# A tuned two-block transformer kernel: another order of quarters ahead of the first seven-product block, weight splits moved to ScalarE, small matmuls in a row, first tiles in front

## The chip, the cores and the metric

The kernel runs on one core of a Trainium2 chip. The metric is device time in microseconds. A core has five engines with instruction queues of their own: TensorE (PE, matmul), VectorE (DVE), ScalarE (ACT), GpSimd (POOL) and SyncE (SP, which only issues DMAs here). Each engine executes its queue in order, and the queues meet through semaphores. 0.2% of this kernel's time is 5.3 us.

## What is computed

Two transformer blocks over 1024 tokens of width 1024, batch 1, all float32.

```python
def first_block(x, ...):
    n = rms_norm(h, attn_norm_w);  proj = n @ w_in          # q, k, v, retention q, k, v, gate
    y_attn = windowed_gqa_sink(rope(norm(aq)), rope(norm(ak)), av, sink)
    y_ret = silu(rg) * rms_norm(bidirectional_retention(rope(rq), rope(rk), rv), ret_norm_w)
    h = h + concat([y_attn, y_ret]) @ w_out
    m = rms_norm(h, ffn_norm_w)
    h = h + (silu(m @ w_gate) * (m @ w_up)) @ w_down        # width 2816

def second_block(h, mem, ...):
    a = rmsnorm(h, g_mix);  proj = a @ w_in                 # 3 x 768 attention, 2 x 512 sgu, 2 x 1024 gates
    y_attn = combine of three dilated windowed attentions
    y_sgu = spatial_gating(...)
    merged = gate0 * (y_attn @ w_branch_attn) + gate1 * (y_sgu @ w_branch_sgu)
    h = h + merged @ w_out
    h = h + cross_attention(rmsnorm(h, g_cross), rmsnorm(mem, g_mem))   # 256 memory tokens
    f = rmsnorm(h, g_ffn)
    h = h + (silu(f @ w_gate) * (f @ w_up)) @ w_down
    return rmsnorm(h, g_final)
```

## The kernel before

**Operands in two parts.** Every large product is made as three matmuls of 128x512: both the weight and the input are split into a high part of type fp32r and the rest (`WH`, `WL`; `XH`, `XL`), and high x high, high x low and low x high are summed in PSUM. So each weight tile costs two splitting operations (high: a copy with rounding; low: a subtraction), on POOL (`split_unit`) or shared between ACT (high) and POOL (low). Inputs are normalised by DVE, split high by ACT and low by DVE or, for the tile numbers in `LOW2` = (5, 7, 9, 10, 11, 13, 14), by POOL. Tile number n is column tile `n % 8` of token half `n // 8`.

**Stages.** In order of time: projections of the first block with windowed attention between them; retention; output projection (`residual`); feed-forward of the first block (`ffn(0, ...)`, first matmuls at about 490 us); the "mix" part of the second block's projections (from about 1137 us); dilated attention, gating and output projection; cross-attention (memory and query units at about 1840 to 1900 us); feed-forward of the second block (`ffn(1, ...)`, from about 1997 us).

**Plain blocks and seven-product blocks.** The feed-forward and the mix part begin with two plain blocks (b = 0, 1): weight block b is cut in quarters A11, A21, A22, A12 of 128x512 and multiplied directly. From b = 2 on a block is done by seven products P1 to P7 instead of eight. They need sums of quarters (`first_sum`: S1 = A21 + A22, into `ACC[:, 1]`; `third_sum`: S3 = A11 - A21, in place of A21; then S2 = S1 - A11 and S4 = A12 - S2, in place of A11 and A12) and sums of the inputs, t1 to t4, which DVE makes and splits with ACT (`input_sums`, semaphores `t_made`, `t_high`, `t_split`). PE takes the products in the order P1, P2, P6, P5, P7, P3, P4, each of 12 matmuls. P1 reads A11, P6 reads S2, P2 reads A12, P5 reads S1, P7 reads S3, P4 reads A22 and P3 reads S4. In the feed-forward, groups of the second weight (`down`) stand between the products from the end of b = 2 on; their raw quarters lie in `XX`.

**The ring of quarters.** Raw quarters are numbered through (`PIECE_OF`, `MIX_PIECE_OF`) and piece r lies in place r % 6: four places in `WRAW`, two in `RAWX`. SP issues the load of piece r once piece r - 6 has been read for the last time (`raw_freed`, `mix_freed`: A11 after S4 and the low part of P6, A21 after the low part of P7, A22 after that of P4, A12 after that of P3; in the plain blocks after the piece's own low part). In the feed-forward the order in which SP issues is sorted by the slot at which the place comes free (`ffn_loads`); in the mix part it is the order of the pieces. SP waits in order, so a load that isn't free yet holds up those behind it. b = 2 has pieces 8 to 11, b = 3 pieces 12 to 15, b = 4 begins with 16.

**POOL's queue at the start of these parts.** `plain` for b = 0: four low parts of weights, then the low parts of the input tiles in `LOW2` (L1010, in the mix part L1182); `plain` for b = 1: four low parts (L986, in the mix part L1131); then for b = 2, at P1: in the feed-forward a wait for `gate_mul` (DVE's first gate), `first_sum` (L1016), `third_sum` (L1022), the low part of P1, S2 (L1050), the low part of P2, and so on; S4 is L1028. After P4 of b = 2: `first_sum` of b = 3, and the sums of the first `down` group (L1064, L1070, L1076). In the mix part the sums of b = 2 come at P1 (L1141, L1147, L1160, L1164) and `mix_first_sum(3)` after P3.

**The cross-attention's weights.** Units of 1024 columns, `CQ_AT[0]` = 73 and `CQ_AT[1]` = 74 for the queries, `MEM_AT[4]` = 72 before them; POOL splits all three, high (L940) and low (L942) for each half. The later units in `EARLY` are shared between ACT, DVE and POOL. `first_units` (L1268, L1269, L1271) starts a pair of units whose inputs are still being made, the second unit three tiles behind the first; `cross_norm` puts the norm's column sums (`norm_sums`, L1284) and its spread over the partitions (`norm_spread`, L1305) between those tiles.

**The very start.** ACT converts three halves of the first two weight units (L2136), then makes `XH` of the first input tiles (L2097, `x_highs`); POOL makes the weights' low parts (L933) and DVE `XL` (L3014).

**The spreads of retention.** `r_spreads(n)` (L1520) spreads the head norms over the partitions, four matmul records for each n; n = 4 to 7 stand between tiles of the output projection's second half (`second_half`), one before each of kt = 0 to 3. DVE then normalises (`r_norms`, L3237, L3239), ACT makes `XH` and DVE `XL` (L3012) of the tiles kt = 4 to 7.

Of the kernel before, what the change touches and what calls it, by code (L numbers as in the profile page):

```python
# [77 lines left out]
EARLY = [MEM_AT[5], CQ_AT[2], MEM_AT[6], MEM_AT[7], CQ_AT[3]]  # L78

# [26 lines left out]
QUARTERS = ("A11", "A21", "A22", "A12")  # L106
GROUPS = ("P1", "P2", "P6", "P5", "P7", "P3", "P4")
# [74 lines left out]
MIX_PIECE_OF = [("plain" if b < 2 else "fast", b, q) for b in range(MIX_BLOCKS) for q in QUARTERS]  # L182
# [11 lines left out]
PIECE_OF = [("plain" if b < 2 else "fast", b, q) for b in range(FT) for q in QUARTERS]  # L194
# [157 lines left out]
def program(nc, xT, memT, ws, vec, cst, rope, bias, wsp, bsg, outT):  # L352
# [6 lines left out]
    with ctx:  # L359
# [564 lines left out]
        def _(pool):  # L924
# [63 lines left out]
            def plain(f, b, u0):  # L988
# [17 lines left out]
                if b == 0:  # L1006
                    for n in LOW2:
                        pool.wait_ge(x_high, (XS_F1, XS_F2)[f] + n + 1)
                        xh, xl = plain_input(n % 8, n // 8)
                        pool.tensor_tensor(xl, scaled_input(n % 8, n // 8), xh.bitcast(F32), ALU.subtract).then_inc(x_low2, 1)  # L1010

            def first_sum(f, b):
                pool.wait_ge(w_low, W_LOW_AT[f] + (SLOT["fast", b - 1, "P5"] + 1 if b > 2 else 8))
                raw_loaded(pool, f, "fast", b, "A21")
                raw_loaded(pool, f, "fast", b, "A22")
                pool.tensor_tensor(S1, raw_of("fast", b, "A21"), raw_of("fast", b, "A22"), ALU.add).then_inc(w_sum, 1)  # L1016
# [13 lines left out]
            def fast(f, b, name):  # L1030
# [3 lines left out]
                if b == 2 and name == "P1":  # L1034

                    pool.wait_ge(gate_mul, 44 * f + 1)
                    first_sum(f, b)
                    third_sum(f, b)
# [110 lines left out]
            def mix_group(b, name):  # L1149
# [3 lines left out]
                if b == 2 and name == "P1":  # L1153
                    mix_first_sum(b)
                    mix_third_sum(b)
# [9 lines left out]
                if name == "P3" and b + 1 < MIX_BLOCKS:  # L1165
                    mix_first_sum(b + 1)
# [4 lines left out]
            for kind, b, name in MIX_SEQ:  # L1171
# [6 lines left out]
                else:  # L1178
                    for n in LOW2:
                        pool.wait_ge(x_high, XS_GMIX + n + 1)  # L1180
                        xh, xl = plain_input(n % 8, n // 8)
                        pool.tensor_tensor(xl, scaled_input(n % 8, n // 8), xh.bitcast(F32), ALU.subtract).then_inc(x_low2, 1)  # L1182
            i = U_FFN1 // 2
# [8 lines left out]
            with pool.Fori(i + 1, EARLY[0] // 2) as i:  # L1192
                for j in range(2):
                    split_unit(i, j)
            split_unit(EARLY[0] // 2, 0)
# [21 lines left out]
        def _(pe):  # L1217
# [321 lines left out]
            def second_half(h, kt):  # L1539
# [3 lines left out]
                if h == 1 and kt < 4:  # L1543
                    r_spreads(4 + kt)
# [424 lines left out]
            def cross_norm(h, kt):  # L1969
                if (h, kt) == (0, 2):  # L1970
# [106 lines left out]
        def _(act):  # L2077
# [55 lines left out]
            for j, q in ((0, 1), (1, 0), (1, 1)):  # L2133
                act.wait_ge(raw_in[j], 16)
                c = slice(512 * q, 512 * q + 512)
                act.activation(WH[:, j, c], WRAW[:, j, c], ACT.Copy).then_inc(one_made, 1)  # L2136

            def x_highs(q):

                act.wait_ge(h_part[q] if q else x_in, 16)  # L2140
                for i in range(4):
                    if (q, i) == (0, 2):
                        act.wait_ge(h_part[0], 16)
# [759 lines left out]
            norm_high(3, 2, 4)  # L2903
            norm_root(3, 1)
            memory_value(4)
            norm_high(3, 4)
            def first_part_high(u):
                i, j = u // 2, u % 2
                act.wait_ge(raw_in[j], 16 * i + 16)
                act.wait_ge(full[2 * j + 1], i)  # L2910
                act.activation(WH[:, j, 0:HALF], WRAW[:, j, 0:HALF], ACT.Copy).then_inc(early_high, 1)
# [74 lines left out]
        def _(dve):  # L2986
# [35 lines left out]
            def norm_step(k, gain, n):  # L3022

                if n < 16:
                    kt, h = n % 8, n // 8
                    if n == 5:
# [773 lines left out]
            norm_step(3, V_GCROSS, 2)  # L3800
            add_squares(3, 15, 1)
            for n in range(3, 17):
                norm_step(3, V_GCROSS, n)

            for n, u in enumerate(EARLY):
                dve.wait_ge(early_high, n + 1)
# [149 lines left out]
```

## Time and profile before

| what | value |
|---|---|
| median of 3 runs | 2663.57 us (2662.53 to 2663.82) |
| the profiled execution's own time | 2663.69 us |
| its span | 2661.9 us |
| PEld, DVE, ACT, POOL busy | 81%, 67%, 42%, 60% |
| chain that ended last | PE 93%, DVE 3%, POOL 1%, issue 1%, ACT 1% |
| mean DMA rate | 65 GB/s |
| `h_spill<-H`, ACT's queue, one issue of 4096 KB | 12.9 us to landing |

The span runs from the first instruction to the last; busy shares are of the span. An engine whose share is near 100% sets the time unless its records hide waits; the chain names what each moment of the span was waiting for. PE's share stands in the rows below.

### The profile page before, as it was taken

How to read it: one execution, taken by the hardware profiler on the slowest of the kernel's cores; microseconds unless marked ns; L12 is line 12 of the kernel's file. 1: busy time of each engine (PE TensorE's matmuls, PEld its weight loads, DVE VectorE, ACT ScalarE, POOL GpSimd, SP SyncE). 2: the span in 40 equal slices, each digit the busy share in tenths (PEclk: the TensorE clock that was granted, in tenths of full speed). 3: DMA queues.
4: the chain of work that ended last, by engine and by line, in shares of the span. 5: the costliest groups of instructions: out<-in, count | busy, mean ns of one | idle time of the engine just before them, and what ended most of it. 6: DMA issues, size and time to landing. Idle time of an engine off the chain costs nothing.

```text
span 2661.9 us, 36644 instructions
## 1 busy us (share of the span) xinstructions
PE 2630.7 (99%) x13442; PEld 2145.0 (81%) x13442; DVE 1777.1 (67%) x2505; ACT 1110.7 (42%) x2152; POOL 1584.5 (60%) x1167
## 2 busy tenths in 40 slices
PE   8999999999999999999999999999999999999998
PEld 6777787878888888878888888888887788888887
DVE  7776775687777777781132447773469877777777
ACT  6644432344444434454443335211445444434443
POOL 3232243478888878667732233557325888878884
PEclk9999999999999999999999999999999999999999
DMA  3111102111121211133211011342101111211112
GB/s 141 33 32 33 45 21 93 55 60 59 57 64 60 64 60 57 55 131 111 85 48 47 25 41 56 134 166 72 64 33 43 58 59 60 72 56 56 60 52 84
DMA packets 110924, 172.98 MB, mean 65 GB/s; under 512 B 7968, under 2 KB 61728, under 8 KB 108576
## 3 DMA queue, kind: packets, MB, share of 16 engines
q1 hardware_dynamic: 100416, 133.20, 15.7%
q10 hardware_dynamic: 10336, 37.49, 3.7%
q8 instruction: 108, 1.77, 0.3%
q14 instruction: 64, 0.52, 0.1%
HBM read 154.93 MB, written 15.73 MB: 64 GB/s over the span
## 4 chain that ended last, share of the span: by engine, by line
PE 93%; DVE 3%; POOL 1%; issue 1%; ACT 1%; DMA 0%; SPq 0%; DVEq 0%; ACTq 0%; POOLq 0%
PE PS L1573 14%; PE PS L1575 14%; PE PS L1574 14%; PE PS L1232 10%; PE PS L1234 9%; PE PS L1233 9%; PE PS L1865 2%; PE PS L1866 2%; PE PS L1867 2%; PE PS L1268 1%; PE PS L1271 1%; PE PS L1269 1%; PE PS L1341 1%; PE PS L1607 1%; PE PS L1367 1%
## 5 line engine op out<-in xcount | busy, mean ns | idle before, releaser
L940 POOL TENSOR_TENSOR WH<-WRAW,CST 128x512 fp32r<-128x512 f32 x150 | 170.9, 1139 | 611.5 <-PE PS L1234 541.3
L1232 PE MATMUL PS<-XH,WH 128*128 128x512 f32 x960 | 395.0, 411 | 0.4 <-DVE XL L3812 0.4
L3509 DVE TENSOR_TENSOR H<-H,PS 128x512 f32<-128x512 f32 x560 | 366.4, 683 | 41.9 <-PE PS L1575 41.8
L1234 PE MATMUL PS<-XH,WL 128*128 128x512 f32 x960 | 376.2, 392 | 0.0
L1233 PE MATMUL PS<-XL,WH 128*128 128x512 f32 x960 | 375.5, 391 | 0.0
L986 POOL TENSOR_TENSOR WL<-WRAW,WH 128x512 fp32r<-128x512 f32 x174 | 260.1, 1496 | 91.1 <-ACT WH L2378 78.0
L986 POOL TENSOR_TENSOR WL<-XX,WH 128x512 fp32r<-128x512 f32 x148 | 197.4, 1335 | 101.9 <-ACT WH L2378 101.5
L1573 PE MATMUL PS<-XH,WH 128*128 128x512 f32 x640 | 249.8, 390 | 1.8 <-ACT ACC L2496 1.4
L1574 PE MATMUL PS<-XL,WH 128*128 128x512 f32 x640 | 249.4, 390 | 0.0
L1575 PE MATMUL PS<-XH,WL 128*128 128x512 f32 x640 | 249.4, 390 | 0.0
L1574 PE MATMUL PS<-PL,WH 128*128 128x512 f32 x624 | 243.2, 390 | 0.0
L1232 PEld LDWEIGHTS PS<-XH,WH 128*128 128x128 f32 x960 | 180.7, 188 | 57.0 <-issue 22.5
L1573 PE MATMUL PS<-PH,WH 128*128 128x512 f32 x576 | 225.0, 391 | 0.7 <-issue 0.7
L1575 PE MATMUL PS<-PH,WL 128*128 128x512 f32 x576 | 224.5, 390 | 0.0
L1234 PEld LDWEIGHTS PS<-XH,WL 128*128 128x128 f32 x960 | 180.4, 188 | 39.3
L942 POOL TENSOR_TENSOR WL<-WRAW,WH 128x512 fp32r<-128x512 f32 x150 | 201.7, 1344 | 11.8
L1233 PEld LDWEIGHTS PS<-XL,WH 128*128 128x128 f32 x960 | 181.1, 189 | 31.5 <-issue 0.5
L1573 PE MATMUL PS<-TR,WH 128*128 128x512 f32 x480 | 187.7, 391 | 3.2 <-DVE ACC L3486 1.7
L1574 PE MATMUL PS<-TR,WH 128*128 128x512 f32 x480 | 187.1, 390 | 0.0
L1575 PE MATMUL PS<-TR,WL 128*128 128x512 f32 x480 | 187.1, 390 | 0.0
L3430 DVE TENSOR_TENSOR PL<-PV,PH 128x512 fp32r<-128x512 f32 x140 | 144.8, 1036 | 38.7 <-ACT PH L2408 38.7
L2408 ACT ACTIVATE PH<-PV 128x512 fp32r<-128x512 f32 x140 | 87.9, 628 | 141.5 <-PE PS L1575 86.1
(456 smaller groups left out, 6087.7 us busy)
## 6 DMA issues: line engine op xcount, KB each, us to landing
WRAW<-ws SPq DMA_DIRECT2D x84, 512.0 KB, 3.4
WRAW<-ws SPq DMA_DIRECT2D x148, 256.0 KB, 2.6
XX<-ws SPq DMA_DIRECT2D x108, 256.0 KB, 2.7
RAWX<-ws SPq DMA_DIRECT2D x68, 256.0 KB, 2.6
gate_spill<-TG ACTq DMA_DIRECT2D x28, 256.0 KB, 2.1
H<-xT ACTq DMA_DIRECT2D x2, 2048.0 KB, 9.6
h_spill<-H ACTq DMA_DIRECT2D x1, 4096.0 KB, 12.9
THB<-gate_spill ACTq DMA_DIRECT2D x4, 1024.0 KB, 5.3
```

The source lines that it names most:

```text
L940: pool.tensor_tensor(WH[:, j, c], WRAW[:, j, c], ONES[:, 0:1].to_broadcast((P, 512)), ALU.mult).then_inc(hi_split, 1)
L942: pool.tensor_tensor(WL[:, j, c], WRAW[:, j, c], WH[:, j, c].bitcast(F32), ALU.subtract).then_inc(unit_split, 1)
L986: pool.tensor_tensor(WLS[:, at], weight(s), WHS[:, at].bitcast(F32), ALU.subtract).then_inc(w_low, 1)
L1232: pe.matmul(out, WH[:, j, w], rh(kt), start=(n == 0), stop=False)
L1233: pe.matmul(out, WH[:, j, w], rl(kt), start=False, stop=False)
L1234: last = pe.matmul(out, WL[:, j, w], rh(kt), start=False, stop=(n == len(kts) - 1))
L1573: pe.matmul(PS[:, bank], WHS[:, at, w], xh, start=start and not on, stop=False, skip_group_check=on)
L1574: pe.matmul(PS[:, bank], WHS[:, at, w], xl, start=False, stop=False, skip_group_check=on)
L1575: return pe.matmul(PS[:, bank], WLS[:, at, w], xh, start=False, stop=stop, skip_group_check=on)
L2408: act.activation(PH[:, n % 2], value(name), ACT.Copy).then_inc(hid_high, 1)
L3430: dve.tensor_tensor(part(name), value(name), PH[:, n % 2].bitcast(F32), ALU.subtract).then_inc(hid_low, 1)
L3509: dve.tensor_tensor(x, x, PS[:, 4 + t], ALU.add).then_inc(h_added, 1)
```

## The change

1. `piece_order`: the quarters of block b = 2 are numbered and loaded in the order A22, A21, A11, A12 (before: A11, A21, A22, A12), in both feed-forwards and the mix part.
2. `first_sum(f, 2)` and `mix_first_sum(2)` move forward in POOL's queue, behind the low part of input tile 7 in the plain block b = 0. They wait for the norm's column sums (`col_sum`) and for A21 and A22. In the mix part, `mix_first_sum(3)` moves from behind P3 to behind P4.
3. In the cross-attention, ACT makes three of the four high halves of units 73 and 74 (`QUERY_HIGHS[1:]`), between its `XH` tiles 2 and 3; POOL keeps one high half and the four low halves. The column sums of the second token half are taken before kt = 4 instead of kt = 2, DVE's last addition of squares comes two tiles later, and its reciprocal at n = 6 instead of 5.
4. `r_spreads(4)` to `r_spreads(7)` stand in a row before kt = 0.
5. At the start ACT makes the first two `XH` tiles before it converts the two halves of the second weight unit.

```diff
+QUERY_HIGHS = [(u, q) for u in CQ_AT[:2] for q in range(2)]
...
+def piece_order(b):
+
+    return ("A22", "A21", "A11", "A12") if b == 2 else QUARTERS
...
-MIX_PIECE_OF = [("plain" if b < 2 else "fast", b, q) for b in range(MIX_BLOCKS) for q in QUARTERS]
+MIX_PIECE_OF = [("plain" if b < 2 else "fast", b, q) for b in range(MIX_BLOCKS) for q in piece_order(b)]
...
-PIECE_OF = [("plain" if b < 2 else "fast", b, q) for b in range(FT) for q in QUARTERS]
+PIECE_OF = [("plain" if b < 2 else "fast", b, q) for b in range(FT) for q in piece_order(b)]
...
                         pool.tensor_tensor(xl, scaled_input(n % 8, n // 8), xh.bitcast(F32), ALU.subtract).then_inc(x_low2, 1)
+                        if n == 7:
+                            first_sum(f, 2)
...
             def first_sum(f, b):
-                pool.wait_ge(w_low, W_LOW_AT[f] + (SLOT["fast", b - 1, "P5"] + 1 if b > 2 else 8))
+                if b > 2:
+                    pool.wait_ge(w_low, W_LOW_AT[f] + SLOT["fast", b - 1, "P5"] + 1)
+                else:
+                    pool.wait_ge(col_sum, 4 + 6 * f)
...
                 if b == 2 and name == "P1":
                     pool.wait_ge(gate_mul, 44 * f + 1)
-                    first_sum(f, b)
                     third_sum(f, b)
...
                 if b == 2 and name == "P1":
-                    mix_first_sum(b)
                     mix_third_sum(b)
...
-                if name == "P3" and b + 1 < MIX_BLOCKS:
+                if name == "P3" and 2 < b < MIX_BLOCKS - 1 or name == "P4" and b == 2:
                     mix_first_sum(b + 1)
...
+                        if n == 7:
+                            mix_first_sum(2)
...
-            with pool.Fori(i + 1, EARLY[0] // 2) as i:
+            with pool.Fori(i + 1, CQ_AT[0] // 2) as i:
                 for j in range(2):
                     split_unit(i, j)
-            split_unit(EARLY[0] // 2, 0)
+            split_unit(CQ_AT[0] // 2, 0)
+            for u, q in QUERY_HIGHS:
+                i, j, c = u // 2, u % 2, slice(512 * q, 512 * q + 512)
+                if (u, q) == QUERY_HIGHS[0]:
+                    pool.wait_ge(raw_in[j], 16 * i + 16)
+                    pool.wait_ge(full[2 * j + 1], i)
+                    pool.tensor_tensor(WH[:, j, c], WRAW[:, j, c], ONES[:, 0:1].to_broadcast((P, 512)), ALU.mult).then_inc(hi_split, 4)
+                    pool.wait_ge(hi_split, 4 * i + 2 * j + 4)
+                else:
+                    pool.wait_ge(early_high, QUERY_HIGHS.index((u, q)))
+                pool.tensor_tensor(WL[:, j, c], WRAW[:, j, c], WH[:, j, c].bitcast(F32), ALU.subtract).then_inc(unit_split, 1)
...
-                if h == 1 and kt < 4:
-                    r_spreads(4 + kt)
+                if (h, kt) == (1, 0):
+                    for n in range(4, 8):
+                        r_spreads(n)
...
-                if (h, kt) == (0, 2):
+                if (h, kt) == (0, 4):
                     norm_sums(3, 1)
...
-            for j, q in ((0, 1), (1, 0), (1, 1)):
+            def first_weights(j, q):
                 act.wait_ge(raw_in[j], 16)
                 c = slice(512 * q, 512 * q + 512)
                 act.activation(WH[:, j, c], WRAW[:, j, c], ACT.Copy).then_inc(one_made, 1)
+            first_weights(0, 1)
...
                     if (q, i) == (0, 2):
+                        first_weights(1, 0)
+                        first_weights(1, 1)
                         act.wait_ge(h_part[0], 16)
...
-            norm_high(3, 2, 4)
+            norm_high(3, 2, 3)
+            for u, q in QUERY_HIGHS[1:]:
+                first_part_high(u, q)
+            norm_high(3, 3, 5)
             norm_root(3, 1)
             memory_value(4)
-            norm_high(3, 4)
+            norm_high(3, 5)
...
-                    if n == 5:
+                    if n == 6:
                         norm_inverse(k, 1)
...
-            norm_step(3, V_GCROSS, 2)
-            add_squares(3, 15, 1)
-            for n in range(3, 17):
+            for n in range(2, 17):
                 norm_step(3, V_GCROSS, n)
+                if n == 4:
+                    add_squares(3, 15, 1)
```

## Rows read from the trace of the kernel before

**Rows 1.** The page, part 1: busy time and share of the span.

```profile
PE 2630.7 (99%) x13442; PEld 2145.0 (81%) x13442; DVE 1777.1 (67%) x2505; ACT 1110.7 (42%) x2152; POOL 1584.5 (60%) x1167
```

**Rows 2.** Waits of PE, whole span: us in total, times, longest us.

```profile
PE PS L1268 <- ACT XH L2097: 8.5, 1, 8.5
```

**Rows 3.** PE by windows: stretch, its us, PE busy (count), clock, DMA share, GB/s.

```profile
545.00:580.00 35.00, 32.16 (x136) 1.00 0.21 69
```

**Rows 4.** PE by windows, the very start.

```profile
8.50:14.90 6.40, 5.94 (x12) 1.00 1.04 389
14.90:22.90 8.00, 8.00 (x37) 1.00 0.87 331
```

**Rows 5.** Timeline, the start: start us, us, engine, line, [idle before <- releaser].

```profile
6.59 1.15 ACT L2136 ACTIVATE WH<-WRAW 128x512 fp32r<-128x512 f32 x2 [0.89 <-DMA WRAW<-ws]
7.65 1.32 ACT L2097 ACTIVATE XH<-H,VEC 128x512 fp32r<-128x512 f32 x2
...
10.11 0.79 PE L1271 MATMUL PS<-XL,WH 128*128 128x512 f32 x1 [0.42 <-DVE XL L3014]
```

**Rows 6.** Timeline, spreads of retention and the last XL behind them.

```profile
396.04 1.89 PE L1520 MATMUL PS<-ROPE,CST 128*64 128x512 f32 x8
...
410.20 1.08 PE L1520 MATMUL PS<-ROPE,CST 128*64 128x512 f32 x4
...
421.82 0.69 DVE L3012 TENSOR_TENSOR XL<-RQ,XH 128x512 fp32r<-128x512 f32 x1 [0.70 <-ACT XH L2097]
```

**Rows 7.** Timeline of POOL in the first feed-forward, blocks 2 and 3.

```profile
530.45 1.29 POOL L1016 TENSOR_TENSOR ACC<-WRAW,RAWX 128x512 f32<-128x512 f32 x1 [7.68 <-DVE SQ L3418]
...
535.88 1.53 POOL L986 TENSOR_TENSOR WL<-WRAW,WH 128x512 fp32r<-128x512 f32 x1 [2.70 <-ACT WH L2378]
...
551.88 2.98 POOL L986 TENSOR_TENSOR WL<-RAWX,WH 128x512 fp32r<-128x512 f32 x2
555.49 1.67 POOL L1016 TENSOR_TENSOR ACC<-WRAW 128x512 f32<-128x512 f32 x1 [0.63 <-DVE SQ L3418]
...
566.88 1.74 POOL L986 TENSOR_TENSOR WL<-WRAW,WH 128x512 fp32r<-128x512 f32 x1
```

**Rows 8.** Timeline of DVE and PE, same stretch.

```profile
555.94 1.78 DVE L3447 TENSOR_TENSOR PV<-SQ,PV 128x512 f32<-128x512 f32 x1
...
560.07 0.50 PE L1573 MATMUL PS<-TR,WH 128*128 128x512 f32 x1 [0.87 <-DVE ACC L3486]
...
568.76 0.47 PE L1573 MATMUL PS<-XH,WH 128*128 128x512 f32 x1 [0.24 <-POOL WL L986]
```

**Rows 9.** DMA issue at 554.9 us: size, us to landing.

```profile
RAWX<-ws SPq DMA_DIRECT2D x1, 256.0 KB, 4.2
```

**Rows 10.** DMA issue at 2062.1 us, the same piece in the second feed-forward.

```profile
RAWX<-ws SPq DMA_DIRECT2D x1, 256.0 KB, 3.1
```

**Rows 11.** Timeline of POOL and PE in the mix part, first plain block.

```profile
1152.00 1.27 POOL L1182 TENSOR_TENSOR XL<-SC,XH 128x512 fp32r<-128x512 f32 x1 [3.36 <-ACT XH L2097]
1155.68 1.29 POOL L1182 TENSOR_TENSOR BXL<-SC,BXH 128x512 fp32r<-128x512 f32 x1 [2.40 <-ACT BXH L2097]
...
1157.27 0.39 PE L1832 MATMUL PS<-BXL,WH 128*128 128x512 f32 x1
```

**Rows 12.** DMA issue at 1147.0 us, piece 9 of the mix part.

```profile
WRAW<-ws SPq DMA_DIRECT2D x1, 256.0 KB, 10.3
```

**Rows 13.** DMA issue at 1203.2 us, the first after P4's low part.

```profile
RAWX<-ws SPq DMA_DIRECT2D x1, 256.0 KB, 3.4
```

**Rows 14.** Timeline of POOL and PE in the mix part, blocks 2 and 3.

```profile
1197.73 0.51 PE L1865 MATMUL PS<-TR,WH 128*128 128x512 f32 x1 [1.57 <-DVE TR L3399]
...
1204.39 1.30 POOL L1131 TENSOR_TENSOR WL<-WRAW,WH 128x512 fp32r<-128x512 f32 x1
...
1209.54 0.39 PE L1865 MATMUL PS<-XH,WH 128*128 128x512 f32 x1
```

**Rows 15.** Timeline of PE, the cross-attention's first query units.

```profile
1862.91 0.50 PE L1268 MATMUL PS<-XH,WH 128*128 128x512 f32 x1 [0.63 <-POOL WL L942]
```

More of the change, by code:

```diff
@@ L2900, in _, with first_part_high @@
                     act.activation(MH[:].rearrange("p a b -> p (a b)"), XX[:], ACT.Copy).then_inc(mem_high, 1)
-            norm_high(3, 2, 4)
+            def first_part_high(u, q=0):
+                i, j, c = u // 2, u % 2, half(q)
+                act.wait_ge(raw_in[j], 16 * i + 16)
+                act.wait_ge(full[2 * j + 1], i)
+                act.activation(WH[:, j, c], WRAW[:, j, c], ACT.Copy).then_inc(early_high, 1)
+            norm_high(3, 2, 3)
+            for u, q in QUERY_HIGHS[1:]:
+                first_part_high(u, q)
+            norm_high(3, 3, 5)
             norm_root(3, 1)
             memory_value(4)
-            norm_high(3, 4)
[L2907 to L2911, printed above, removed]
+            norm_high(3, 5)
             for n in range(4):
@@ L3798, in _ @@
                     last.then_inc(mem_val, 1)
-            norm_step(3, V_GCROSS, 2)
-            add_squares(3, 15, 1)
-            for n in range(3, 17):
+            for n in range(2, 17):
                 norm_step(3, V_GCROSS, n)
+                if n == 4:
+                    add_squares(3, 15, 1)
             for n, u in enumerate(EARLY):
-                dve.wait_ge(early_high, n + 1)
+                dve.wait_ge(early_high, 3 + n + 1)
                 dve.tensor_tensor(WL[:, u % 2, 0:HALF], WRAW[:, u % 2, 0:HALF], WH[:, u % 2, 0:HALF].bitcast(F32),
```

## Prediction

> **What bounds the kernel.** The page's busy line first: PE is busy for 2630.7 of 2661.9 us [rows 1], so the kernel is a string of matmuls, and what an edit can win is PE's idle time, 31 us in all. Two lumps of it are not for this change to win whole: the 8.5 us before the first matmul [rows 2] and the tail. Next the waits of PE and its windows: the idle time between sits where a stage begins. The start of the first feed-forward's fast blocks has 35.0 - 32.16 = 2.8 us [rows 3], the second feed-forward repeats it, the mix part has 1.6 us in one wait [rows 14], and the cross-attention some 1.3, of which the longest stands in [rows 15]. A term of this forecast is therefore a microsecond or two, and its sign depends on who is late next.
>
> **The start (edit 5).** ACT converts two weight halves from 6.59 us and only then makes XH at 7.65, since the input had just come (its own idle time is none there) [rows 5]; so XH itself hardly moves (0.1 us). What moves is POOL: those two halves' low parts no longer run beside the first XL, and PE waits for that XL, until 10.11 [rows 5]. A DVE operation on SBUF beside a POOL one takes 1.78 us [rows 8] where the plain ones beside nothing take 0.69 [rows 6], so the first XL comes 1.0 us earlier. PE then works at its lower rate: 12 matmuls in 6.4 us up to 14.9 us, about 35 in the next 8 [rows 4]; 0.43 us each are 512 columns at 1.2 GHz, 0.23 us nearly that at 2.4 GHz, although the clock column has no lower grant for that stretch. If the clock still rises at 14.9, a start 1.0 us earlier puts two more matmuls before the rise, and each is worth 0.23 us afterwards: -0.5 us, not -1.0. Bounds: -1.1 (the rise comes with the work) and +0.2 (the third and fourth XL now meet POOL's low parts). The Trainium skill ("TensorE: Matmul & The Clock Gate", Part 1) says that the monitor behind the clock runs free of the kernel's start, so that the rise is not tied to the first matmul; by that rule the term could be -0.5 in one run and -1.1 in another, and no row here tells which.
>
> **The spreads in a row (edit 4).** Four records between other matmuls take 1.08 us, eight in a row 1.89 [rows 6]: four more cost 0.81 to 0.85, so sixteen in a row take 3.6 where four times four take 4.1. Each break also costs PE about 0.1 us on either side (a first matmul behind a wait or another kind lasts 0.50 instead of 0.39 [rows 8, 14]), and three of four breaks go. Together 0.5 + 0.6 = 1.1 us. But the last tile's XL starts at 421.82 and ends at 422.5 [rows 6], at the end of a ladder of DVE and ACT steps that begins with the first spread at 410.20 and doesn't get earlier. PE uses that XL at 422.95 now; 1.1 us earlier it would wait for it. So 0.3 us is won. Bounds -1.1 and 0.
>
> **The cross-attention (edit 3).** POOL loses three conversions of about 1.04 us. PE waits 0.63 us for one of its low parts [rows 15], and two shorter waits before it are DVE's and ACT's. But three ACT conversions of 0.6 us now stand before the XH of tile 3, and the low halves that remain on POOL still run beside DVE's XLs. I place tile 2's XL about 1 us earlier, tile 4's and 5's at the same time as now, since the column sums with ACT's root and DVE's reciprocal move behind them. The spread that follows starts 0.2 to 0.6 us earlier: -0.4 us. Bounds: -1.9 (all waits and their refills) and +0.7 (three conversions, less the 1.1 us of slack that XH of tile 3 has).
>
> **The first sum (edits 1 and 2), first feed-forward.** What goes: one POOL operation of 1.29 us at 530.45, behind 7.68 us of idle time. POOL idles for another 2.70 us afterwards, until ACT delivers at 535.88 [rows 7]. So nothing waits for it, and taking it away wins nothing; at its new place (about 505 us) POOL is idle too. What is added is a load that comes later. Piece 14 (A22 of b = 3) lies in place 14 % 6 = 2, which was A11's of b = 2, free at S4; it is now A22's, free at the low part of P4, POOL's second operation of the pair at 551.88, so at 554.86 [rows 7]. In SP's sorted order it goes last of seven, where a load issued at that moment takes 4.2 us [rows 9]: landed at 559.07. POOL's `first_sum(3)` reads it, now at 555.49 [rows 7]: 3.6 us late, and behind it in POOL's queue stand the two `down` sums and the low parts for which PE waits, with 0.24 us of idle time at 568.76 [rows 8], where POOL's string has no slack. How much reaches PE? The string from 555.49 to the low part at 566.88 is 8 operations, most of them 1.57 to 1.75 us because DVE works beside them [rows 7]; free they take 1.29 [rows 7]. While POOL waits for the load, DVE is free and runs ahead (its 1.78 us operation at 555.94 [rows 8] becomes 0.7, and PE's wait of 0.87 us at 560.07 [rows 8] goes), so that most of the string then runs uncontended: I count three operations contended and five free, -1.7 us, and 0.7 us of slack at the `down` group behind. 3.6 - 1.7 - 0.7 = +1.2 us. Bounds +0.3 (all eight free) and +3.4 (all contended as now).
>
> **Second feed-forward.** The same, but there the load takes 3.1 us [rows 10], 1.1 less: +0.1 us, bounds -0.2 and +2.4.
>
> **The mix part.** (a) `mix_first_sum(2)` now stands behind the low part at 1152.00, with idle time until 1155.68 [rows 11]. It needs pieces 8 and 9. Piece 9 is issued at 1147.0 and takes 10.3 us [rows 12], beside the 4 MB spill of H: landed at 1157.3. So POOL waits for the load until 1157.3, then 1.29 for the sum and 1.29 for the low part of tile 9, which is ready at 1159.9; PE uses it at 1157.27 [rows 11]. That is 2.6 us, 2.7 with the refill. Behind it PE has 1.57 us of idle time at 1197.73, until DVE's t-splits arrive [rows 14], which the delay fills: +1.1 us, if DVE's chain stays where it is (one POOL operation less beside its sums, but all the others later). Bounds 0 and +2.7. (b) Piece 14 again: issued when P4's low part ends at about 1203.1, 3.4 us to land [rows 13], then `first_sum(3)`, the third sum and P1's low part, 3 x 1.29: 1210.4 instead of 1205.7 (1204.39 + 1.30); PE starts P1 at 1209.54 [rows 14]. 0.9 and a refill of 0.1: +1.0 us. Bounds 0 (POOL's queue is shorter and PE later by a) and +2.2. (a) is the risk that the moved sum creates: a wait for a load in front of low parts that PE needs at once.
>
> **The sum.** -0.5 - 0.3 - 0.4 + 1.2 + 0.1 + 1.1 + 1.0 = +2.2 us, against the profiled execution: 2663.7 + 2.2 = 2665.9. That execution lies 0.1 us above the median of the three runs (2663.57), so the forecast for a median is 2665.8 us. +2.2 us is 0.08%. What this kernel's measurement can tell from no change is about 0.2%, 5.3 us, so I call this no change.
>
> **Rivals.** (A) *The late load decides.* POOL's string in both feed-forwards keeps its contended durations, the delay of `first_sum(3)` reaches PE whole (+3.4 and +2.4), and in the mix part DVE's chain moves with PE (+2.7, +2.2): 10.7, less 1.2 for the other edits: +9.5, 2673.1 us. It decides from about 1.5 us per feed-forward on. For it: POOL's string reaches PE with 0.24 us of idle time now; against: DVE's operations run in the gap. Slower by 0.36%. (B) *The covers hold and the small edits pay.* The loads' delays vanish in slack, and start (-1.0), spreads (-1.1), cross-attention (-1.9) come through: -4.0, with 1.0 left for the mix part: -3.0, 2660.6 us. For it: PE's idle time is there to win; against: each of the three has its next waiter named above. Faster by over 0.2% it would be only from -5.3 us on. (C) *Nothing arrives.* The first sum had 2.70 us of slack where it stood and the new load order costs nothing that PE sees; the first sum is not the wait at all: 2663.4 us.
>
> **How the numbers follow.** Forecast 0.45, A 0.15, B 0.2, C 0.2. The time is 2665.8. The range takes in B and C and the lower half of the way to A: 2660.3 to 2670.2. Slower by over 0.2% (2668.9 and more): A whole and a little of the forecast's upper bounds, 0.17. Faster by over 0.2% (below 2658.2): B with every bound at its end, 0.07. Within: 0.76.
>
> **What would show it.** PE starts with its third matmul near 9.4 us and no 0.42 us wait. The spreads stand as 16 records in about 3.6 us, with a new PE wait of about 0.5 us for XL near 421.8. POOL has no L1016 between 522 and 530 us; a gap of about 4 us ended by a DMA stands before `first_sum(3)` in both feed-forwards, and PE's idle time in the stretch of [rows 3] grows by about 1 us. In the mix part a POOL gap ended by `WRAW<-ws` near 1157, then a PE wait of about 2.6 us for BXL, and a shorter or no wait for L3399 near 1198; a PE wait for POOL before P1 of b = 3. Wrong would be: no PE wait at BXL (then piece 9 landed earlier or the order of the queue isn't what I read), or PE's idle time in the feed-forward's stretch smaller than before.

## The result, and the profile after

| | before | after |
|---|---|---|
| median, the two timed side by side | 2664.29 us (13 runs) | 2670.45 us (13 runs) |
| ratio to before | 1 | 1.0021, 95% interval 1.0014 to 1.0028 |
| the profiled execution | 2663.69 us, span 2661.9 | 2669.91 us, span 2668.1 |

The change makes the kernel slower, by 6.2 us by the medians and 5.6 us by the ratio. Page part 1 of the kernel after answers to [rows 1]: PE is busy for 2.5 us more, though it runs the same 13442 matmuls.

```profile
PE 2633.2 (99%) x13442; PEld 2148.4 (81%) x13442; DVE 1766.5 (66%) x2505; ACT 1112.2 (42%) x2155; POOL 1574.6 (59%) x1164
```

Waits of PE of the kernel after (line waited at, releaser: us in total, times, longest). Two kinds are new, 6.3 and 3.3 us:

```profile
PE PS L1597 <- POOL WL L994: 6.3, 2, 3.2
PE PS L1856 <- POOL BXL L1193: 3.3, 1, 3.3
```

PE by windows (stretch, its us, PE busy and count, granted clock, DMA share, GB/s) answers to [rows 3] and says what makes PE busier: behind each new wait the granted clock is half, 1.2 instead of 2.4 GHz.

```profile
545.00:580.00 35.00, 30.78 (x126) 0.95 0.23 72
...
559.90:563.10 3.20, 0.01 (x1) 0.94 0.00 0
563.10:566.50 3.40, 3.40 (x9) 0.55 0.00 0
566.50:570.00 3.50, 3.50 (x17) 1.00 0.00 0
1158.00:1161.30 3.30, 0.05 (x1) 0.81 0.01 2
1161.30:1164.80 3.50, 3.44 (x8) 0.50 0.00 0
1164.80:1168.30 3.50, 3.50 (x12) 0.70 0.02 5
2071.90:2075.10 3.20, 0.06 (x2) 0.96 0.01 3
2075.10:2078.50 3.40, 3.40 (x9) 0.54 0.00 0
```

What the clock takes from the matmuls is read there: 3.4 us at 0.55 and 0.54 lose 1.5 and 1.6 us; in the mix part 3.5 us at 0.50 and 3.5 at 0.70 lose 1.8 + 1.1 = 2.8 us. How much of it is left at the end of a stage depends on the waits behind. The matmuls of 128x512 start 0.43 us apart in such a stretch and 0.23 us apart outside it.

**The first feed-forward.** POOL's timeline answers to [rows 7] (first_sum is L1029, third_sum L1035, the low part L994):

```profile
557.07 1.29 POOL L1029 TENSOR_TENSOR ACC<-WRAW 128x512 f32<-128x512 f32 x1 [4.21 <-DMA WRAW<-ws]
558.32 1.28 POOL L1076 TENSOR_TENSOR XX<-XX 128x512 f32<-128x512 f32 x1
559.75 1.53 POOL L1082 TENSOR_TENSOR XX<-XX 128x512 f32<-128x512 f32 x1
561.24 1.71 POOL L994 TENSOR_TENSOR WL<-XX,WH 128x512 fp32r<-128x512 f32 x1
```

Its load, the DMA issue at 552.9 us (size, us to landing), and PE:

```profile
WRAW<-ws SPq DMA_DIRECT2D x1, 256.0 KB, 4.0
```

```profile
563.10 0.76 PE L1597 MATMUL PS<-PH,WH 128*128 128x512 f32 x1 [3.21 <-POOL WL L994]
```

PE had ended P4 early, because its wait for DVE before P4 (0.87 us in [rows 8]) was gone, and waited at the first matmul of the first `down` group. That is for the fourth operation of POOL's string, the low part at 561.24, four operations earlier than the place where [rows 8] show PE waiting for POOL. The second feed-forward does the same (its load takes 3.9 us, its wait is 3.14).

**The mix part**, POOL (first_sum L1153) and PE (answering to [rows 11]), and further on the sum of block 3:

```profile
1152.60 1.27 POOL L1193 TENSOR_TENSOR XL<-SC,XH 128x512 fp32r<-128x512 f32 x1 [3.35 <-ACT XH L2121]
1158.35 1.27 POOL L1153 TENSOR_TENSOR ACC<-WRAW 128x512 f32<-128x512 f32 x1 [4.48 <-issue]
1159.58 4.64 POOL L1193 TENSOR_TENSOR BXL<-SC,BXH 128x512 fp32r<-128x512 f32 x3
...
1209.60 1.29 POOL L1153 TENSOR_TENSOR ACC<-WRAW 128x512 f32<-128x512 f32 x1 [2.90 <-DMA WRAW<-ws]
```

```profile
1161.36 0.79 PE L1856 MATMUL PS<-BXL,WH 128*128 128x512 f32 x1 [3.31 <-POOL BXL L1193]
```

Piece 9, issued at 1147.6 us, takes 10.4 us here (10.3 in [rows 12]), so it lands at 1158.0. The profile books POOL's 4.48 us before the sum as issue, not as a wait for a DMA; that it is the load is read from the landing, and spill_later below shows it. PE's wait of 1.57 us at the t-splits [rows 14] is gone, swallowed by the delay.

**The small edits.** The third matmul of the start, the spreads, PE's wait behind them and the last XL, and the two waits that are left in the cross-attention's first units (answering to [rows 5, 6, 15]):

```profile
9.51 0.63 PE L1294 MATMUL PS<-XL,WH 128*128 128x512 f32 x1
```

```profile
408.86 3.65 PE L1543 MATMUL PS<-ROPE,CST 128*64 128x512 f32 x16
```

```profile
420.50 0.50 PE L1291 MATMUL PS<-XH,WH 128*128 128x512 f32 x1 [0.28 <-ACT XH L2121]
```

```profile
420.47 0.69 DVE L3044 TENSOR_TENSOR XL<-RQ,XH 128x512 fp32r<-128x512 f32 x1 [0.70 <-ACT XH L2121]
```

```profile
1861.88 0.47 PE L1291 MATMUL PS<-XH,WH 128*128 128x512 f32 x1 [0.53 <-POOL WL L1218]
1865.08 0.50 PE L1291 MATMUL PS<-XH,WH 128*128 128x512 f32 x1 [0.22 <-POOL WL L1218]
```

**Where the time went**, for this kernel and for those of the next section. The matmuls come in the same order in all traces, so each can be paired with its own in the trace of before (in keep_busy without the matmuls that it adds). A number is how much later (+) PE starts a matmul at the end of the stretch than it did before, less the same at the stretch's beginning (read at 20, 440, 540, 580, 1140, 1215, 1845, 1880, 2050 and 2095 us; the first column from zero; the spreads from 400 us).

| kernel | start | spreads | FFN 1 | mix | cross | FFN 2 | ratio to before (95%) |
|---|---|---|---|---|---|---|---|
| after | -1.36 | -0.26 | +2.20 | +3.80 | -1.13 | +2.26 | 1.0021 (1.0014 to 1.0028) |
| undo_order | -1.28 | -0.25 | -0.02 | -0.02 | -1.14 | 0.00 | 0.9990 (0.9981 to 0.9999) |
| sums_back | -1.59 | -0.25 | +2.75 | +0.72 | -1.10 | +2.74 | 1.0015 (1.0006 to 1.0024) |
| order_b3 | -1.71 | -0.25 | -0.10 | +2.97 | -1.11 | -0.35 | 0.9998 (0.9989 to 1.0007) |
| spill_later | -1.62 | -0.26 | +2.37 | -0.35 | -1.09 | +1.04 | 1.0006 (0.9997 to 1.0015) |
| both | -0.73 | -0.26 | -0.42 | -0.34 | -1.14 | -0.34 | 0.9983 (0.9974 to 0.9992) |
| both_sums_back | -1.41 | -0.28 | +0.03 | +0.83 | -1.11 | +0.02 | 0.9993 (0.9984 to 1.0002) |
| both_old_start | +0.03 | -0.26 | -0.13 | -0.28 | -1.14 | -0.34 | 0.9987 (0.9978 to 0.9996) |
| keep_busy | -1.32 | -0.25 | +1.80 | +2.80 | -1.12 | +2.65 | 1.0014 (1.0005 to 1.0023) |
| stalls | -1.20 | 0.00 | +4.80 | +0.02 | +0.01 | +2.60 | 1.0024 (1.0015 to 1.0034) |
| cross_only | -0.25 | 0.00 | 0.00 | +0.02 | -1.12 | +0.02 | one run, no ratio |
| spreads_only | -0.47 | -0.24 | -0.03 | -0.01 | +0.01 | +0.03 | one run, no ratio |

The row of after sums to +5.5 us; 0.7 us more lies behind 2600 us, where the traces scatter by up to 1.6 us (cross_only has that much there, from no edit of its own).

### The profile page after: what moved, and what is told of

Same layout as the page of the kernel before. It is cut to its first block, busy times and chain, and to the rows that moved or that the text cites. A ratio compares the mean times of both kernels' runs of the same rounds, so it can differ in the third digit from the quotient of the medians.

```text
span 2668.1 us, 36637 instructions
## 1 busy us (share of the span) xinstructions
PE 2633.2 (99%) x13442; PEld 2148.4 (81%) x13442; DVE 1766.5 (66%) x2505; ACT 1112.2 (42%) x2155; POOL 1574.6 (59%) x1164
## 4 chain that ended last, share of the span: by engine, by line
PE 95%; DVE 2%; POOL 1%; DMA 1%; issue 1%; ACT 1%; ACTq 0%; DVEq 0%; POOLq 0%
PE PS L1597 14%; PE PS L1599 14%; PE PS L1598 14%; PE PS L1255 10%; PE PS L1257 9%; PE PS L1256 9%; PE PS L1891 2%; PE PS L1890 2%; PE PS L1889 2%; PE PS L1291 1%; PE PS L1631 1%; PE PS L1625 1%; PE PS L1294 1%; PE PS L1626 1%; PE PS L1292 1%; PE PS L1364 1%
## 5 line engine op out<-in xcount | busy, mean ns | idle before, releaser
L948 POOL TENSOR_TENSOR WH<-WRAW,CST 128x512 fp32r<-128x512 f32 x146 | 165.4, 1133 | 602.7 <-PE PS L1257 535.6
L994 POOL TENSOR_TENSOR WL<-WRAW,WH 128x512 fp32r<-128x512 f32 x172 | 257.0, 1495 | 86.6 <-ACT WH L2406 73.2
L994 POOL TENSOR_TENSOR WL<-XX,WH 128x512 fp32r<-128x512 f32 x148 | 196.9, 1332 | 103.7 <-ACT WH L2406 103.3
L950 POOL TENSOR_TENSOR WL<-WRAW,WH 128x512 fp32r<-128x512 f32 x146 | 195.5, 1339 | 11.5
L994 POOL TENSOR_TENSOR WL<-RAWX,WH 128x512 fp32r<-128x512 f32 x84 | 128.6, 1532 | 41.3 <-ACT WH L2406 41.3
```

The lines of the kernel that those rows point to most:

```text
L948: pool.tensor_tensor(WH[:, j, c], WRAW[:, j, c], ONES[:, 0:1].to_broadcast((P, 512)), ALU.mult).then_inc(hi_split, 1)
L950: pool.tensor_tensor(WL[:, j, c], WRAW[:, j, c], WH[:, j, c].bitcast(F32), ALU.subtract).then_inc(unit_split, 1)
L994: pool.tensor_tensor(WLS[:, at], weight(s), WHS[:, at].bitcast(F32), ALU.subtract).then_inc(w_low, 1)
```

## The experiments

**undo_order: edits 3 to 5 alone.**

```diff
-    return ("A22", "A21", "A11", "A12") if b == 2 else QUARTERS
+    return QUARTERS
...
-                        if n == 7:
-                            first_sum(f, 2)
...
                     pool.wait_ge(gate_mul, 44 * f + 1)
+                    first_sum(f, b)
                     third_sum(f, b)
```

(the mix part's sums likewise)

> The kernel after with its edits 1 and 2 taken back (loads in the old order, first sums at P1, the mix part's first_sum(3) behind P3); edits 3 to 5 stay. Theory (the late loads make all of the loss): no PE wait over 1.6 us, clock 1.0 from 14 to 2653 us, and what stays is the three small gains that the comparison of the two traces shows: start -1.35, spreads -0.3, cross-attention -1.1 = -2.7 us against before, ratio to before about 0.9990, some 9 us under the kernel after. Rival (the small edits cost something themselves, and the loss is not only in the loads): at or over the kernel before, ratio 1.0000 or more.

Measured 2661.84 us, 0.9990: the three small edits win 2.7 us by the trace, and all of the loss is in edits 1 and 2.

**sums_back: the new load order with the sums at P1.** Both feed-forwards keep the new order, only `first_sum(f, 2)` and `mix_first_sum(2)` return to where they were.

> The kernel after with the first sums of block 2 back at P1 in both feed-forwards and the mix part; the new load order and the rest stay. Theory (in the feed-forwards the load order costs, in the mix part the moved sum does): the 3.2 us PE waits near 560 and 2072 us and their stretches at a granted clock of 0.5 stay as they are, the 3.3 us PE wait for BXL near 1158 us and its stretch at half clock go: -3.7 us against the kernel after, ratio to before about 1.0007. Rival 1 (the moved sum also costs in the feed-forwards): their waits become shorter and the time falls by 6 us or more. Rival 2 (the sum's place does not matter, the load order alone costs): the mix part loses its 3.3 us elsewhere, the time stays within 1 us of the kernel after.

Measured 1.0015. In the feed-forwards the waits stay (3.14 and 3.12 us), so there the order costs; in the mix part the wait for BXL is gone with the moved sum. The time forecast (1.0007) was too low: against the kernel after, each feed-forward is 0.5 us later, and the mix part keeps 0.7 us over before, with PE waiting 0.39 us for POOL before P1 of block 3.

```profile
1150.00:1170.00 20.00, 19.80 (x94) 1.00 0.49 194
```

**order_b3: another piece is the late one,** A12, which is wanted later than A22.

```diff
+def ffn_piece_order(b):
+    return ("A21", "A22", "A12", "A11") if b == 3 else piece_order(b)
...
-PIECE_OF = [... for q in piece_order(b)]
+PIECE_OF = [... for q in ffn_piece_order(b)]
```

> The kernel after, with the quarters of block 3 in both feed-forwards numbered A21, A22, A12, A11, so that the piece that needs the place freed last is A12 (wanted at S4) and not A22 (wanted by the first sum). Theory (piece 14, landed at 556.91 us, is what holds POOL's string): POOL's gap of 4.21 us ended by a DMA before the first sum of block 3 falls below 1 us, the 3.2 us PE waits near 560 and 2072 us go, the granted clock stays 1.0 there, and each feed-forward wins back 2.3 to 3 us (3.2 of wait and 1.5 of half clock, less the 0.9 + 1.0 us that PE's waits behind had absorbed): ratio to before about 1.0004. Rival (A11 now comes as late as A22 did, and the third sum of block 3 waits in its place): the wait moves some 4 us later at the same size, and the time stays.

Measured 0.9998 (1.0004 expected); against the kernel after, the trace gives -2.3 and -2.6 us for the two feed-forwards. POOL's timeline of this kernel: no wait for a load before the sum (L1034), 0.90 us for one of `XX` behind it; PE then waits 1.00 us instead of 3.21.

```profile
553.09 1.67 POOL L1034 TENSOR_TENSOR ACC<-WRAW 128x512 f32<-128x512 f32 x1 [0.63 <-DVE SQ L3455]
555.66 1.54 POOL L1081 TENSOR_TENSOR XX<-XX 128x512 f32<-128x512 f32 x1 [0.90 <-DMA XX<-ws]
```

```profile
560.72 0.47 PE L1602 MATMUL PS<-PH,WH 128*128 128x512 f32 x1 [1.00 <-POOL WL L999]
```

The rival fell: A11 is wanted only by `third_sum(3)`, which stands four operations later, and its load is there by then.

**spill_later: the 4 MB spill out of the way of piece 9.**

```diff
-            act.dma_start(H_DRAM, H[:]).then_inc(h_out, 16)
             for n in range(4, 16):
                 mix_input_high(n)
+                if n == 6:
+                    act.dma_start(H_DRAM, H[:]).then_inc(h_out, 16)
```

> The kernel after, with the 4 MB spill of H issued some 5 us later, behind XH of input tile 6 of the mix part, so that it does not stand beside the load of piece 9. Theory (piece 9, issued at 1147.6 us, lands only at 1157.9 because it shares the DMA engines with the spill): it lands by 1152 us, the first sum ends before BXH of tile 9 is made (1156.2 us), the 3.3 us PE wait for BXL and the half clock behind it (1161 to 1168 us) go: -3.7 us against the kernel after, with 1.6 us of PE wait for the t-splits near 1198 us back. Rival (the load waits behind piece 8 or the wait is for something else): no change. Second rival (the spill, moved, now hits the loads or ACT's wait for it at 1163 us): the gain is half of that or less.

Measured 1.0006. The DMA issues between 1145 and 1149 us, then POOL:

```profile
h_spill<-H ACTq DMA_DIRECT2D x1, 4096.0 KB, 11.8
WRAW<-ws SPq DMA_DIRECT2D x1, 256.0 KB, 2.6
```

```profile
1153.63 1.29 POOL L1153 TENSOR_TENSOR ACC<-WRAW 128x512 f32<-128x512 f32 x1
1156.06 1.29 POOL L1193 TENSOR_TENSOR BXL<-SC,BXH 128x512 fp32r<-128x512 f32 x1 [1.14 <-ACT BXH L2121]
```

The same load takes 2.6 us instead of 10.4, and the sum runs with no wait. The mix part gives -0.35 instead of +3.80; at the t-splits PE waits 0.87 us, where 1.6 had been expected. This kernel showed something else: its two feed-forwards have the same PE wait, and only one loses its clock.

```profile
559.60:562.70 3.10, 0.00 (x0) 1.00 0.00 0
562.70:566.50 3.80, 3.78 (x12) 0.67 0.00 0
...
2067.60:2070.70 3.10, 0.00 (x0) 1.00 0.01 3
2070.70:2074.20 3.50, 3.47 (x15) 1.00 0.00 0
```

The difference in the table, +2.37 against +1.04, is what the half clock leaves at the end of that stage: 1.3 us. In the kernel after the two feed-forwards differ by 0.06 us.

**stalls: the kernel before, with nothing changed but POOL's time.**

```diff
+                if b == 3:
+                    for n in range(3 - f):
+                        pool.tensor_tensor(S1, raw_of("fast", b, "A21"), raw_of("fast", b, "A22"), ALU.add).then_inc(y_out, 1)
+                        pool.wait_ge(y_out, 3 * f + n + 1)
                 pool.tensor_tensor(S1, ...).then_inc(w_sum, 1)
```

> The kernel before, with the sum S1 of block 3 made four times over in the first feed-forward and three times in the second, one after the other on POOL (no load, no order and no input is changed). 1.3 to 1.7 us each, less 0.8 us of slack: PE waits 3.1 to 4.3 us for the first down group near 563 us and 1.8 to 2.6 us near 2070 us. Theory (a PE stall of over 3 us takes the clock down, whatever makes it): a stretch of 3.4 us at a granted clock of 0.5 in the first (+1.5 us of time), none in the second. Rival (the clock falls because of what the DMA or POOL does in the kernel after): clock 1.0 in both.

Measured 1.0024. PE waits 4.08 us, then 2.20:

```profile
561.90:565.90 4.00, 0.00 (x0) 1.00 0.00 0
565.90:569.30 3.40, 3.36 (x8) 0.53 0.00 0
...
2074.00:2076.20 2.20, 0.03 (x1) 1.00 0.00 0
2076.20:2079.70 3.50, 3.07 (x13) 1.00 0.01 2
```

The clock falls without the load, the new order or anything else of the change: PE's idleness is enough. Its price here is smaller than the 1.5 us expected: the table's 4.80 - 2.60 = 2.2 us is nearly all the longer wait, 4.08 - 2.20 = 1.9 us, so the half clock leaves 0.3. Behind the shorter wait PE, at full rate, waits for POOL's next low parts again (0.43 and 0.23 us), and behind the longer one, at half rate, it does not.

**keep_busy: matmuls in the gap.**

```diff
                     if n == 0:
                         pe.wait_ge(hid_made, 44 * f + 4)
+                        for m in range(12):
+                            xh = fast_input("P1", m % 4)[0]
+                            pe.matmul(PS[:, 4], xh[:, 0:P], xh, start=True, stop=True)
```

> The kernel after, with 12 matmuls of 128x512 whose results nobody reads put in front of PE's wait for the first down group's low part in each feed-forward (they take 2.8 us of a 3.2 us wait). Theory (the clock falls because PE is idle): both waits shrink to about 0.4 us, the clock stays 1.0 in the feed-forwards, each gives back the 1.5 us that half clock cost: -3 us against the kernel after, ratio to before about 1.0010; the mix part keeps its 3.3 us wait and its half clock. Rival 1 (the drop has nothing to do with PE's idle time): the clock falls all the same, time unchanged or up by the matmuls' overhang. Rival 2 (the slow stretch is hidden by later slack, so it costs nothing): clock 1.0, but time unchanged.

Measured 1.0014. The clock is 1.00 behind both waits, which are 1.08 and 1.92 us:

```profile
563.80:567.30 3.50, 3.50 (x15) 1.00 0.00 0
...
2075.20:2078.70 3.50, 3.48 (x15) 1.00 0.00 0
...
1157.70:1161.00 3.30, 0.06 (x1) 1.00 0.01 2
1161.00:1164.50 3.50, 3.50 (x11) 0.65 0.02 5
```

The forecast of the clock holds, that of the time does not: FFN 1 gives back 0.4 us and FFN 2 costs 0.4 more. The late load took 4.7 and 5.6 us here instead of 4.0 and 3.9, 0.7 and 1.7 us more, beside the 1.3 us that the half clock left in spill_later. That fits FFN 2 and leaves 0.2 us over in FFN 1. Why the load took longer stays open. The mix part's +2.80 is 1.0 us below the kernel after because its half clock was shorter this time, which no edit asked for.

**both: the two mends together.**

> The kernel after with the two mends together: block 3 of the feed-forwards in the order A21, A22, A12, A11, and the spill of H issued behind XH of tile 6 of the mix part. Theory (they take away separate waits and add up): the PE waits near 560, 1158 and 2068 us are below 1.1 us each and the clock is 1.0 from 14 us on; against the kernel before -1.4 (start), -0.5 (spreads and what precedes them), -0.4 (first feed-forward), -0.3 (mix part), -1.2 (cross-attention), -0.3 = -4 us: ratio 0.9985, some 1.5 us under the kernel with edits 1 and 2 undone. Rival (the new order is worth nothing once its loads are on time): the same as with edits 1 and 2 undone, 0.9990.

Measured 2660.36 us, 0.9983: the fastest of all, 3.8 us under the kernel before beside it; the theory's 0.9985 and -4 us held. That it also beats undo_order (0.9990) rests on the traces, since the two intervals overlap: -0.4, -0.3 and -0.3 us in the three stages that edits 1 and 2 touch, against 0.0 in all three. No wait of PE between the first one and 2600 us is over 0.9 us, and the clock stays up:

```profile
545.00:580.00 35.00, 32.55 (x138) 1.00 0.24 73
1150.00:1170.00 20.00, 19.80 (x91) 1.00 0.56 224
2056.00:2091.00 35.00, 32.87 (x140) 1.00 0.28 89
```

**both_sums_back: what the moved sum is worth once no load is late.** Both mends, the sums at P1 as in sums_back.

> The kernel with both mends, with the first sums of block 2 back at P1 in both feed-forwards and the mix part. Question: what the moved sum is worth once no load is late. Theory A (the forecast's: POOL idles 2.70 us behind the sum where it stood, so moving it wins nothing): the places of PE at 580, 1215 and 2095 us relative to those ahead of each stage stay within 0.1 us of the kernel with both mends. Theory B (the moved sum lets the t-splits come earlier: PE's wait for them near 547 us is 0.31 us in every trace with the early sum and 0.69 us in every one without): each feed-forward loses 0.4 us and the mix part 0.3 to 0.8 us (its wait for the t-splits back to 1.6 us), ratio to before about 0.9987.

Measured 0.9993. By the table the early sum wins 0.4 us in each feed-forward and 1.2 in the mix part, 2 us. It wins them at DVE's t-splits. The last t-splits of the first feed-forward, in this kernel and then in the kernel with both mends:

```profile
545.66 1.90 DVE L3432 TENSOR_TENSOR TR<-XX,TR 128x512 fp32r<-128x512 f32 x3 [0.60 <-ACT TR L2448]
```

```profile
546.03 1.90 DVE L3437 TENSOR_TENSOR TR<-XX,TR 128x512 fp32r<-128x512 f32 x3 [0.42 <-ACT TR L2453]
```

The second kernel stands 0.76 us later at 540 us (-0.98 against -1.74), so its splits are 0.4 us earlier in their place, and PE waits 0.31 us for them at 547 us instead of 0.69; in the mix part it is 0.81 us at 1195 us instead of 1.56. Against the kernel before, edits 1 and 2 together still win only 0.3 us in the mix part, since P1 of block 3 costs 0.8 us in both kernels. Which of the DVE operations beside POOL makes the 0.4 us was not separated.

**both_old_start, cross_only, spreads_only.** Edit 5 undone in the best kernel; edit 3 alone and edit 4 alone in the kernel before.

> The kernel with both mends, but with edit 5 undone (ACT converts the second unit's two halves ahead of the first two XH, as before). Question: what the start edit is worth, since the traces so far put the 11th matmul or so 0.6 to 1.4 us earlier with it, and one trace without it (the one with the sums repeated) 0.8 us earlier too. Theory A (the edit wins what the forecast said, 0.5 us, the rest is scatter of the loads and of the clock's rise): at 20 us this kernel is 0 to 1 us behind the one with both mends. Theory B (it wins the 1.3 us that before and after differ by): 1.3 us behind at 20 us, ratio to before 0.9989 instead of 0.9983. From 100 us on both traces run alike in either case.

> The kernel before with edit 4 alone. Theory (the spreads in a row win 0.3 us, bounded by the last tile's XL): after 425 us it is 0.3 us (0.2 to 0.5) ahead of the kernel before relative to its place at 400 us, with a PE wait of 0.3 to 0.5 us near 421 us. Rival (the whole 1.1 us arrives): 1 us ahead. It has the old start too, so it gives one more sample of the old start: 0 to 0.8 us ahead of the kernel before at 20 us if that scatters.

> The kernel before with edit 3 alone. Theory (the weight halves moved to ACT win by themselves): 1.1 us (0.8 to 1.3) ahead at 1870 us relative to its place at 1850 us. Rival (1.1 us of gain in the comparison came from the stalls ahead of it, by which POOL and ACT had more time): 0.4 us or less, as forecast. One more sample of the old start as well.

Without edit 5 the kernel takes 2661.35 us, 0.9987, and stands 0.76 us behind at 20 us: within theory A, and the ratio doesn't tell A from B. Edit 3 wins 1.12 us alone, edit 4 0.24, as within the whole change: both theories held. The start scatters. Five traces without edit 5 (before, both_old_start, cross_only, spreads_only, stalls) stand at 0, +0.03, -0.25, -0.47, -1.20, mean -0.4; eight with it from -0.73 to -1.71, mean -1.4. So edit 5 is worth about 1.0 us, though single pairs of traces say anything from +0.5 to -1.7. The third matmul alone comes 0.6 us earlier (9.51 against 10.11); the rest is in when the matmuls become 0.23 us apart. The kernel stalls, which has the old start, shows one source: its first XL was not late that time, and its third matmul has no wait.

```profile
9.28 0.63 PE L1275 MATMUL PS<-XL,WH 128*128 128x512 f32 x1
```

## Why the prediction was right or wrong

The mechanism stood in the prediction, its size did not: +2.2 us were forecast, 6.2 came, between the forecast and rival A. No change by 0.2% was called likeliest; the ratio is at that bound, and its interval (1.0014 to 1.0028) leaves out 1. The median of 2670.45 us lies 0.25 us above the range, but the kernel before, timed beside it, was 0.7 us slower than the 2663.57 us from which the forecast started; 2663.57 x 1.0021 = 2669.2 us lies inside. That it does is in part luck: the half clock, which no term had, was offset by (b), which did not come, and by the small edits, which won 2.7 us instead of 1.2. Rival A's own sign, over 1.5 us per feed-forward, came true, but not its reason: 0.9 us of the delay was won back by freer POOL operations, and 1.5 us is clock. Rivals B and C fell with undo_order, where the kernel without edits 1 and 2 is the faster one.

- **Start:** -0.5 forecast, about -1.0 measured over thirteen traces, inside the term's bounds. The third matmul at 9.51 us without its wait was right. The step "if the clock still rises at 14.9" was wrong in the profiled execution: the matmuls are 0.23 us apart from 13.6 us on, behind twelve slower ones as before, so in this trace the rise came with the work. Over the thirteen traces the slower ones number 10 to 14, once 7, so that is no rule.
- **Spreads:** -0.3 forecast, -0.24 to -0.28 in every trace that has edit 4. PE's new wait there is 0.28 us for XH, where 0.5 for XL had been named, and the last XL comes at 420.47, which is 1.35 us earlier, as all of this trace is since the start: by the ladder as it was said.
- **Cross-attention:** -0.4 forecast, -1.1 measured, alone and in company. Mis-sized by 0.7: the 0.63 us wait of [rows 15] is gone, and so are the waits for ACT and DVE ahead of it (0.48 and 0.16 us), which I had mostly given back to the three conversions on ACT. Two waits for POOL's low parts stand there instead, 0.53 us at an earlier matmul and 0.22. The waits differ by 0.5 us; the other 0.6 was not separated.
- **First feed-forward:** +1.2 forecast, +2.2 measured. The late landing was right to 0.2 us: relative to the end of P4's low part the load comes at the time named, 4.2 and measured 4.0 us behind the issue, and `first_sum(3)` is 3.6 us late against a PE that is 2.0 us ahead (557.07 - 555.49 + 2.0). What failed is the step "-1.7 uncontended, -0.7 slack": it was counted down to the low part of [rows 8] at 568.76, eight operations, while PE, freed of its own waits, already needed the fourth operation. There only 0.9 us had been won back, and the slack was 0.5 us: 3.6 - 0.9 - 0.5 = 2.2. The cover was spent before the place for which it was counted. Then comes what no term had, the half clock, 1.5 us. Through the stretch: -0.4 (PE's wait for t-splits at 546.7 us), +2.2 at 563.1 us, +1.5 of half clock, -1.0 in waits behind that are gone.
- **Second feed-forward:** +0.1 forecast, +2.3 measured. I carried over the 3.1 us of [rows 10]; the load takes 3.9 at its new place in time. With that the same as above, the clock again on top.
- **Mix part (a):** +1.1 forecast, +3.8 measured. Landing (1157.3 forecast, 1158.0 measured, PE's wait 2.6 and 3.31) was right. The missing term is the half clock, 2.8 us. The cover of 1.57 us at the t-splits was used, as said.
- **Mix part (b):** +1.0 forecast, 0 measured in the kernel after: PE comes 4.4 us late to P1 of block 3 and no longer needs it early. (a) and (b) can't both be paid. Where (a) is mended, (b) shows, in both as a wait of 0.47 us (waits of PE between 1205 and 1210 us) and 0.8 us by the pairing, near the forecast's 1.0. In both_sums_back the wait is 0.55 us and the delay again 0.8. The wait in both:

```profile
PE PS L1894 <- POOL WL L1148: 0.5, 1, 0.5
```

- **"Taking the sum away wins nothing":** wrong by 0.4 us in each feed-forward and 1.2 in the mix part. Nothing on POOL waited for that sum, and I looked no further; but DVE's t-splits come earlier without it.

So the largest thing that the sum lacked is the clock: it took 1.5 + 2.8 + 1.6 = 5.9 us from the matmuls. How much of that reached the end was shown only for single stages, 1.3 us in spill_later and 0.3 in stalls; for the mix part no run separates it. In the trace of before no wait behind the first matmul is over 1.6 us, so nothing there shows what a longer one brings, though its start shows both rates; a forecast of a PE wait of 3 us should have carried it as a rival.

## What to carry to other kernels

Reordering a ring of buffers so that one operand comes early makes another one late: list, for each piece, which place it inherits and when that is free, and give the place that frees last to the piece that is wanted last; here that turned +2.2 us per stage into -0.4. Don't move a wait for a load in front of work that the bounding engine needs at once when a bulk transfer stands beside that load. A PE stall of 3.1 to 3.3 us took 4.7 to 6.1 us of PE's time with the half clock behind it, though later waits gave part of that back, so take such stalls apart before trimming short ones.

## What was not expected of the hardware

- Of ten PE stalls of 3.1 to 4.1 us in these traces, nine were followed by a stretch at half clock, one (3.13 us in spill_later) was not; the stalls of 1.0 to 2.2 us never were, and none lay between 2.2 and 3.1. Once, in the mix part of the kernel after, 6.8 us passed before the clock was full again, elsewhere some 3.4.
- The Trainium skill ("TensorE: Matmul & The Clock Gate", Part 1) says that the monitor behind the clock runs free of the kernel. The trace agrees: waits of 3.12 and 3.13 us in one kernel end differently. The untraced runs point the same way: of the 11 runs of sums_back, the six with a mean granted clock of 0.996 took 2669.6 us on average, the two with 0.998 took 2665.8. The kernel before has such runs too, though its trace shows no long wait: 9 of the 90 timed beside the experiments had 0.996 and took 2668.1 us on average, against 2663.9 for the 74 with 0.998. Where their clock fell isn't shown. So a single trace, and each row of the table above, is one draw of the clock. No run varied the place of a stall at a fixed length, so more than that isn't shown.
- A load of 256 KB took 10.4 us behind a 4 MB spill issued 3 us ahead of it, and 2.6 us when the spill was issued later; the spill itself took 13.0 and 11.8 us.
